# A fused decoder layer on one Trainium2 core: the RWKV state chain started earlier among small products, and the S5 output product regrouped by token offset

## What is computed

```python
z = h @ p['w_in']
u_a, p_b, q_c, f_c, i_c, og_c, gate_logits = jnp.split(z, IN_SPLITS, axis=-1)
# S5, 16 groups of 16 channels, 64 complex states each
y = einsum('nlgp,gcp->nlgc', sr, c_re) - einsum('nlgp,gcp->nlgc', si, c_im)
y = gelu(y + d_skip * u)
# RWKV-7, 8 heads of 64, one step per token
sa = einsum('nhvk,nhk->nhv', s, a_t)
s = s * w_t + sa[..., None] * b_t + v_t[..., None] * k_t
y_t = einsum('nhvk,nhk->nhv', s, r_t)
# all three, merged
merged = sum(sigmoid(gate_logits)[i] * (y_i @ w_lift_i))
```

## Time and profile before

| | |
|---|---|
| median of 3 runs | 2260.98 us (2257.70 to 2262.88) |
| profiled execution, own time | 2259.44 us |
| its span | 2257.7 us |
| PE busy, share of span | 2180.0 us, 97% |
| DVE busy | 1154.0 us, 51% |
| ACT busy | 406.3 us, 18% |
| mean granted TensorE clock | 0.988 |

### The profile page before, as it was taken

The page is one execution under the profiler, slowest core; times in us unless marked ns, Lnnn a source line. Parts: engine busy times, 40 slices in busy tenths (PEclk is TensorE's granted clock), DMA queues, the critical chain, the costliest instruction groups (busy, mean ns, idle before and its releaser), DMA issues.

```text
span 2257.7 us, 42337 instructions
## 1 busy us (share of the span) xinstructions
PE 2180.0 (97%) x18743; PEld 1615.2 (72%) x18743; DVE 1154.0 (51%) x1773; ACT 406.3 (18%) x783; POOL 161.9 (7%) x276
## 2 busy tenths in 40 slices
PE   6998999999999999999899998999999999999998
PEld 4665666666566566666556687888888888888887
DVE  5875344252353253344234657656663366657654
ACT  3125121232142142142110003111100011111001
POOL 2620000001002002001000000000000000000000
PEclk8999999999999999999999999999999999999999
DMA  8310132201111111021235322111112311111201
GB/s 302 107 43 10 56 127 96 85 9 53 48 49 59 46 51 56 20 81 36 70 129 205 105 77 76 38 39 40 45 67 89 125 40 39 39 39 53 109 29 78
DMA packets 117540, 161.55 MB, mean 72 GB/s; under 512 B 15890, under 2 KB 87047, under 8 KB 117344
## 3 DMA queue, kind: packets, MB, share of 16 engines
q1 hardware_dynamic: 101568, 132.68, 18.1%
q10 hardware_dynamic: 10992, 15.21, 1.9%
q0 software_dynamic: 4800, 10.97, 1.5%
HBM read 126.24 MB, written 32.59 MB: 70 GB/s over the span
## 4 chain that ended last, share of the span: by engine, by line
PE 94%; DVE 2%; ACT 1%; issue 1%; SPq 1%; DMA 0%; DVEq 0%
PE ps L821 93%; PE ps L825 1%; ACT Y L1865 1%; DVE arena L2167 1%; SPq L515 1%; DVE Y L2170 0%; SPq L532 0%; DMA arena<-in_state_s_dram 0%; DVE Y L2167 0%; ACT arena L1763 0%; DVE arena L2621 0%; DVE arena L2367 0%; ACT hT L2071 0%; ACT L1865 0%; DVE Y L2754 0%
## 5 line engine op out<-in xcount | busy, mean ns | idle before, releaser
L821 PE MATMUL ps<-hT,W 128*128 128x352 f32 (+1 forms) x3472 | 1013.4, 442 | 9.8 <-issue 5.2
L821 PEld LDWEIGHTS ps<-hT,W 128*128 128x128 f32 x3472 | 645.8, 191 | 268.6 <-issue 22.5
L821 PE MATMUL ps<-arena 64*64 64x64 f32 (+5 forms) x8888 | 410.8, 244 | 29.8 <-issue 12.0
L821 PEld LDWEIGHTS ps<-arena 64*64 64x64 f32 (+3 forms) x8888 | 325.6, 140 | 157.8 <-issue 83.0
L821 PE MATMUL ps<-arena,W 128*128 128x264 f32 x1200 | 278.2, 386 | 1.6 <-DVE arena L2167 1.6
L821 PEld LDWEIGHTS ps<-arena,W 128*128 128x128 f32 x1200 | 227.9, 190 | 41.1 <-issue 2.1
L2167 DVE TENSOR_TENSOR Y<-Y,ps 128x528 f32<-128x528 f32 x150 | 105.7, 704 | 276.6 <-PE ps L821 276.1
L2167 DVE TENSOR_TENSOR arena<-arena 128x1056 f32<-128x1056 f32 (+7 forms) x164 | 146.7, 894 | 58.1 <-PE ps L821 43.7
L1763 ACT ACTIVATE Y<-ps 128x528 f32<-128x528 f32 (+1 forms) x96 | 39.9, 415 | 747.9 <-PE ps L821 394.1
L821 PE MATMUL ps<-Y,W 128*128 128x352 f32 (+1 forms) x592 | 166.0, 437 | 4.0 <-DVE Y L2167 4.0
L821 PEld LDWEIGHTS ps<-Y,W 128*128 128x128 f32 x592 | 112.8, 191 | 52.7 <-DVE Y L2167 5.0
(11 more groups left out here) (313 smaller groups left out, 1502.5 us busy)
## 6 DMA issues: line engine op xcount, KB each, us to landing
W<-in_w_up_dram SPq DMA_DIRECT2D x22, 1024.0 KB, 7.1
W<-in_w_ada_dram SPq DMA_DIRECT2D x8, 2048.0 KB, 10.3
W<-in_w_in_dram SPq DMA_DIRECT2D x13, 1024.0 KB, 6.8
gates<-arena ACTq DMA_DIRECT2D x72, 176.0 KB, 1.8
arena<-xres SPq DMA_DIRECT2D x22, 528.0 KB, 5.1
arena<-gates SPq DMA_DIRECT2D x21, 528.0 KB, 3.6
xres<-arena POOLq DMA_DIRECT2D x16, 528.0 KB, 7.2
W<-in_w_ada_dram SPq DMA_DIRECT2D x32, 256.0 KB, 2.8
```

The costliest lines, as they stand in the source:

```text
L821: return nc.tensor.matmul(out, lhsT, rhs, start=start, stop=stop, skip_group_check=True)
```

## The change

S5: `y5` goes over token offsets instead of channel blocks. For offset o it makes a bank in which the row block q (32 rows) belongs to channel block 4*half + q: 12 products with 32 columns of weights, in place of 3 with 128. `y5_gelu` empties each bank by one activation of 128 rows.

RWKV: the chain starts right after the chunk updates and half of the local outputs. The other half, the correction products, `ada_cols`, four gate products, the carried outputs and most of the sample part's first products are spread over the chain's steps. The carried output products of chunk c no longer follow in step c; they come two chunks per step from step 9 on. VectorE adds the correction in four pieces between `carry(5)` and `carry(9)`. Gates that stood in the chain go behind the sample part. ScalarE's copies follow the new order. Two semaphores for loads become one (`mixer_in`), with the counts fitted.

```diff
@@ y5 @@
-                for j in range(4 * half, 4 * half + 4):
+                for o in range(DS):
                     b = misc_bank()
-                    for ri in range(2):
-                        mm(pb[b][:, 0:M], GY[:, ri, j, :, :].rearrange("p l c -> p (l c)"), SS[:, ri, j, 0:M],
-                           ri == 0, False)
-                    mm(pb[b][:, 0:M], FIR[:, j, :, :].rearrange("p o c -> p (o c)"), U4[:, j, :], False, True)\
-                        .then_inc(sem("y5_done"), 1)
+                    for n in range(3):
+                        for q in range(4):
+                            j = 4 * half + q
+                            w_, x_ = ((GY[:, n, j, o, :], SS[:, n, j, 0:M]) if n < 2 else (FIR[:, j, o, :], U4[:, j, :]))
+                            m = mm(pb[b][32 * q:32 * q + 32, 0:M], w_, x_, n == 0, n == 2)
+                    m.then_inc(sem("y5_done"), 1)
@@ chain, tensor @@
+                for c in range(0, 8, 2):
+                    y_part(c)
                 for c in range(1, 16):
...
                     if c == 1:
-                        pe.wait_ge(sem("y_part"), j + 1)
-                        pe.wait_ge(sem("gm_ev"), 2 * j + 2)
-                    m = heads(lambda hp: mm(pb[2 + par_][hp, col64(i)], Sb[hp, c - 1, :], ARp[hp, c, 1, :], False, True))
-                    gates(55 + c, 56 + c)
+                        y_part(8)
+                        y_part(10)
+                    elif c == 2:
+                        y_part(12)
+                        y_part(14).then_inc(sem("y_part"), 1)
+                    elif c == 3:
+                        take(0, 1)
+                        ar_part(0)
+                    elif c == 4:
+                        ar_part(1).then_inc(sem("gm_done"), 1)
...
+                    elif c == 5:
+                        ada_cols(8 + j, 7)
+                    elif c < 9:
+                        gates(46 + c, 47 + c if c < 8 else 56)
+                    else:
+                        if c == 9:
+                            pe.wait_ge(sem("y_part"), j + 1)
+                            pe.wait_ge(sem("ar_ready"), 4 * (j + 1))
+                        y_carried(2 * c - 17)
+                        y_carried(2 * c - 16)
...
+                y_carried(15).then_inc(sem("ry_done"), 1)
...
+                gates(56, 58)
                 pe.wait_ge(sem("dec_made"), 4 * j + 1)
...
-                gates(80, 88)
+                gates(64, 76)
                 pe.wait_ge(sem("ry_ev"), 2 * (j + 1))
...
-                gates(88, 96)
+                gates(76, 96)
@@ vector @@
-                dve.wait_ge(sem("gm_done"), 3 * j + 3)
-                for par_ in range(2):
-                    r = ARp[:, par_:16:2, 1, :]
-                    step(tt(r, pb[par_].rearrange("p (c t) -> p c t", t=RCH), r, ADD), "gm_ev" if par_ else "dve_step")
                 for c in range(1, 16):
                     dve.wait_ge(sem("ds_done"), 15 * j + c)
                     carry(c)
+                    if 5 <= c < 9:
...
+                        step(tt(r, pb[par_][:, 256 * u:256 * u + 256].rearrange("p (c t) -> p c t", t=RCH), r, ADD), "ar_ready")
```

More of the change, by code:

```diff
@@ L1434, in _ @@
-                m.then_inc(sem("dec_done"), 1)
-                give("dec_copied", 0)
-                take(1)
-                for x, src in enumerate((Bp, Kp)):
-                    heads(lambda hp: mm(pb[1][hp, P * x:P * (x + 1)], src[hp, 16, :],
-                                        ARp[hp, 16, :, :].rearrange("p a b -> p (a b)")))
-                heads(lambda hp: mm(pb[1][hp, 2 * P:2 * P + 64], ARp[hp, 16, 0, :], Bp[hp, 16, :]))\
-                    .then_inc(sem("dec_done"), 1)
-                give("dec_made", 1)
@@ L1443, in _ @@
-                take(4)
-                gt4 = pb[4][:, 0:P].rearrange("p (a t) -> p a t", a=2)
-                for n in range(NS):
-                    ts_ = slice(LS * n, LS * (n + 1))
-                    m = heads(lambda hp: mm(gt4[hp, :, ts_], Sin[hp, n, :], ARp[hp, 16, :, ts_]))
-                m.then_inc(sem("dec_done"), 1)
-                give("dec_made", 4)
-                gates(72, 74)
+                        y_part(8)
[8 more added lines that the diff above has]
+                        ar_part(1).then_inc(sem("gm_done"), 1)
+                        readers["ar_ready"] = 4 * j + 3
+                        give("ar_ready", 0, 1)
+                    elif c == 5:
[8 more added lines that the diff above has]
+                        y_carried(2 * c - 16)
@@ new lines, in _ @@
+                    if c == 9:
+                        take(0)
+                        for x, src in enumerate((Vp, Bp, Kp)):
+                            m = heads(lambda hp: mm(pb[0][hp, 64 * x:64 * x + 64], src[hp, 16, :], idS[hp, :]))
+                        m.then_inc(sem("dec_done"), 1)
+                        give("dec_copied", 0)
+                    elif c == 10 or c == 11:
+                        if c == 10:
+                            take(1)
+                        x, src = c - 10, (Bp, Kp)[c - 10]
+                        heads(lambda hp: mm(pb[1][hp, P * x:P * (x + 1)], src[hp, 16, :],
+                                            ARp[hp, 16, :, :].rearrange("p a b -> p (a b)")))
+                        if c == 11:
+                            heads(lambda hp: mm(pb[1][hp, 2 * P:2 * P + 64], ARp[hp, 16, 0, :], Bp[hp, 16, :]))\
+                                .then_inc(sem("dec_done"), 1)
+                            give("dec_made", 1)
+                    elif c > 11:
+                        for n in range(2 * c - 24, 2 * c - 22):
+                            ts_ = slice(LS * n, LS * (n + 1))
+                            m = heads(lambda hp: mm(gt1[hp, :, ts_], Sin[hp, n, :], ARp[hp, 16, :, ts_]))
+                        if c == 15:
+                            m.then_inc(sem("dec_done"), 1)
+                            give("dec_made", 1)
@@ L1467, in _ @@
                 give("dec_made", 1)
[L1468 removed]
+                gates(60, 62)
                 pe.wait_ge(sem("dec_made"), 4 * j + 3)
@@ L1859, in y5_gelu @@
             def y5_gelu(half):
-                for j in range(4 * half, 4 * half + 4):
-                    act.wait_ge(sem("y5_done"), j + 1)
-                    q, src = slice(32 * (j % 4), 32 * (j % 4) + 32), pb[6 + (2 * NJ + j + 1) % 2]
-                    for o in range(DS):
-                        m = nc.scalar.activation(Y[q, j // 4, o::DS], src[32 * o:32 * o + 32, 0:M], ACT.Gelu_apprx_tanh)
-                    m.then_inc(sem("y5_ev"), 1)
+                for o in range(DS):
+                    n = DS * half + o
+                    act.wait_ge(sem("y5_done"), n + 1)
+                    nc.scalar.activation(Y[:, half, o::DS], pb[6 + (2 * NJ + n + 1) % 2][:, 0:M], ACT.Gelu_apprx_tanh)\
+                        .then_inc(sem("y5_ev"), 1)
             for q, fn in enumerate((ACT.Silu, ACT.Sigmoid, ACT.Copy, ACT.Sigmoid)):
```

77 lines of the change are left out of this document (39 added, 38 removed).

## The result

The changed kernel takes 2242.24 us in the median of 4 runs (2237.95 to 2248.92) against 2260.18 us before (4 runs); the ratio is 0.9918, 95% interval 0.9896 to 0.9939. A second set of runs gave 2239.48 us (6 runs) against 2260.92 (17 runs), ratio 0.9907 [0.9892, 0.9922]. It is faster, by 18 to 21 us or 0.8 to 0.9%; the forecast was 2235.1 with 2225 to 2250. The profiled execution took 2240.04 us, 19.4 less than that of before, where the sum said 24.3.

The account below looks back on a forecast made before the run. TensorE's matmul line was taken as the bound, 93% of the chain. S5's 8.2 us plus RWKV's 16.1 (4.0 a pass) made 24.3, from 2259.4 to 2235.1 us; range 2225 to 2250.

Parts of the forecast that it names:

- S5, 8.2 said: S5 output products and transposes: first half gains 2.6 us, second half with transposes 5.6, together 8.2.
- HGRN2 and everything after it move forward together: Behind S5: the number of projection products is unchanged, so the 8.2 us gained in S5 carries through later stages.
- The wait rival: Behind S5, raised with the experiments: a wait comes with HGRN2's earlier start and takes back time; no chance given.
- The step of the chain, 0.85 said: RWKV chain: steps with little filling fall from 1.17 us to a bare latency of 0.85, summed from three pieces.
- The rival of 1.17 us: RWKV chain: latency keeps steps at 1.17 us, costing 14 us in all, total 2249; chance 0.13.
- The wait at the first sample product: RWKV after step 15: TensorE newly waits some 0.6 us for the sample part's first six VectorE operations.
- said were 26.9: RWKV pass, Gm products to the sample part's end: 26.9 us without issue gaps, where the whole stretch took 41.2.
- The issue gap, 0.8 a pass: RWKV runs of small products: TensorE's issue gaps stay a cost, taken as 0.8 us a pass.
- The moved gate products, 9.5 said: RWKV behind the stretch: 16 gate products of a pass moved into long runs at 0.592 us each, 9.5 us.
- The clock no longer drops: RWKV stretch: without the 1.6 us wait the clock stays 1.00, about 0.8 us of each pass's gain.
- The rival in which the thin chain keeps half rate: RWKV steps 1 to 15: clock falls to 1.2 GHz, 11 us a pass, total 2278; chance 0.05.
- The rival with new issue gaps: Whole kernel: the gain goes into new issue gaps or other waits, to 2255 or no gain; chance 0.04.

Follow-up runs that it names:

- s5_only: The kernel before with only the S5 part, narrow products and whole-bank GELUs; RWKV as before: 2256.43 us, ratio 0.9981.
- the second profile: The changed kernel profiled once more with no edit, in the second set of runs: 2239.48 us, ratio 0.9907.
- s5_pad56: The kernel before with the S5 part alone plus 56 idle products ahead of the HGRN2 levels: 2257.25 us, ratio 0.9993.
- fuller: The changed kernel with one more gate product in each of the last two groups ahead of the chain, none in step 6: 2238.78 us, ratio 0.9907.
- pad16: The changed kernel with 16 idle products of four moving columns ahead of the HGRN2 levels: 2234.52 us, ratio 0.9889.

## Why the prediction was right, and where it was off

**Right**: the sign, the range, and the mechanisms. The GELUs went off the path; the wait of 1.6 us for the correction went; the chain steps fell to their latency.

**S5, 8.2 said, 10.0 measured.** The term "scaled to 264 columns that is 0.50 us" a round measured 0.47: the two halves end 0.8 us earlier than said. The transposes took 2.7 instead of 2.9. The rest, 0.9, is a low-clock stretch at 223 to 226 us in the profile of before that the one after hasn't, so the change itself was worth 9.1. "0.66 us by the old row if time goes by columns" was low by up to 0.26 us, and hidden.

**"HGRN2 and everything after it move forward together" failed in part.** The step held every stage's length fixed. Up to pass 0 that was so: the 3.0 us given back in the first profile are lost clock, and the second has none. Behind it s5_only gave back 5.3 of 10.6 us by the end, and in twelve runs at full clock it keeps 3.8 of some 9. An issue gap belongs to a count of instructions and not to a stage, so 144 more records in S5 move each later gap, here to places that cost 3.5 us more from 240 to 1180 us (14.8 against 11.3). The wait rival, one that comes with the earlier start, isn't borne out: waits are 17.7 us against 18.5. Gaps and waits together are 2.7 us of the 5 lost at full clock; the remainder is not accounted for.

**The step of the chain, 0.85 said, 0.79 measured.** The sum of three pieces was right in kind; TensorE's piece with both ways is 0.51, not 0.57. With 11 light steps that is 0.7 us a pass. The rival of 1.17 us is refuted.

**The wait at the first sample product, "some 0.6", measured 0.35.** The tail of 7.3 is unchanged. Gaps left out, a stretch is 26.4 us, 26.0 in the three passes without low clock; said were 26.9.

**The issue gap, 0.8 a pass, measured 2.0.** This is the term that was mis-sized most: 2.66, 2.94, 1.51 and 0.90 us in the four stretches, 1.2 too little a pass, 4.8 in four. The starting value was wrong already: the prediction read "0 to 1.7 us a pass" and took 0.8, where the four stretches of before have 1.14, 1.72, 0.36 and 0.68, mean 1.0. So it forecast fewer gaps for a longer run of small products. Its one reason was the slower pace of steps 1 to 4, "21 instead of 29 products per us". A piece is 64 products in 3.6 us, so every pace above 18 products per us runs dry, 21 too. Rows 6 had half of it: 84 products, a gap.

**The moved gate products, 9.5 said, 9.7 measured** (all that the rest of the kernel grew by, gaps and clock included), so the pass came to 28.4 + 9.7 = 38.1 us against the 37.2 of the sum; RWKV gave 12.4 instead of 16.1.

**"The clock no longer drops" failed** in pass 0 (0.94), and its reason with it: the clock also fell with no idle time ahead, and elsewhere in another execution of the same kernel. The rival in which the thin chain keeps half rate isn't borne out: 1.00 in three passes with steps 1 to 15 as thin as in pass 0 (the second profile loses 1.7, 3.4 and 0.6 us of clock in the stretches of passes 0, 2 and 3, of 26 to 31 us each). So the rule of the Trainium skill (TensorE: Matmul & The Clock Gate, "A second HAM failure mode: psum-queue depth-cycling") has no effect of that size here.

The rival with new issue gaps had a chance of 0.04 and a time up to 2255; it was right in kind, and at a fifth of the gain in size. One of the prediction's own signs of being wrong was issue gaps over 2 us a pass; the mean is 2.0, and two passes are over it. That the sum came as near as it did is in part luck: 4.8 us of gaps above the term, and 3.0 us given back for which there was no term, met an S5 term that was 1.8 us too low (half of that a low clock before) and stretches that were, gaps left out, 1.8 us shorter in sum than said. What was left lay inside the "issue gap doubled" of the range.

## What to carry to other kernels

Where TensorE's list is the bound and holds runs of small products, count instructions as well as time: a run that uses 64 small products in less than 3.6 us is paced by the supply of instructions, and a denser packing of it earns nothing. Any edit that changes the number of instructions moves every later gap, so an edit in one stage has a price in others that no timeline of before shows; give it a range of some 5 us either way. To judge such an edit, bring the borders back to their old place with idle instructions, as s5_pad56 does, and compare times multiplied by the granted clock beside the medians: by that estimate fuller, which looked like nothing, was worth 6.6 us, and pad16, which looked like 5 us, was worth 1. Long products in the middle of a chain stop the gaps but pay for two changes of kind each; put them where they were going to stand anyway.

## What was unexpected in the hardware

- TensorE's instructions came in packets of 16.4 KB, one for each 128 MATMUL records with their weight loads; where gaps stood the packets were 3.6 to 3.9 us apart, with the DMA engines otherwise idle, and each started 1.1 us after a gap's end.
- 16 idle products, 1.8 us of TensorE, moved the later gaps by 32 records against the work and left the kernel no slower; its median was 5 us lower, with intervals that overlap, and about 4 of the 5 were the granted clock.
- Four products of 32 columns side by side cost 0.47 us at 264 moving columns, as much as one wide product (0.47): the round is paid once, though each of the four loads its own weights.
- The granted clock fell to 0.50 after 7 us in which TensorE was busy for 6.91, and at other places in the next execution of the same kernel. What brings it down here stays open.
